# Mixture-of-experts stage: groups ranked by size, the fullest group's two blocks on one set of weights, the smallest group's halves stacked

## The reference

```python
g_sel = argmax(hf @ w_r1 + b_r1)                 # one group of 4 per token
top_p, top_i = top_k(softmax(e_logits[g_sel]), 2) # two of its 4 experts
hid = silu(hf @ w_gate[e]) * (hf @ w_up[e])       # for every expert e, 1024 -> 256
hid = hid * combine[token, e]                     # zero where e was not chosen
out = sum over e of hid @ w_down[e]               # 256 -> 1024
x = x + out
```

## Time and profile before

| | us |
|---|---|
| median of 3 runs | 1083.11 (1082.84 to 1084.38) |
| profiled execution, its own time | 1084.64 |
| its span, first to last instruction | 1082.6 |
| PE busy in the span | 1070.2 (99%) |
| DVE busy | 726.8 (67%) |
| ACT busy | 617.7 (57%) |
| first product of pass 0 starts | 898.57 |
| transposes of pass 19 start | 1073.77 |

### The profile page before, as it was taken

One profiled execution on the slowest core, in us unless ns is written; L12 is line 12 of the kernel. 1 busy time (PEld: TensorE's weight loads), 2 busy tenths in 40 slices (PEclk: granted clock), 3 DMA queues, 4 the chain that ended last, 5 costly groups with the idle time before them and its releaser, 6 DMA issues.

```text
span 1082.6 us, 17152 instructions
## 1 busy us (share of the span) xinstructions
PE 1070.2 (99%) x7044; PEld 957.6 (88%) x7044; DVE 726.8 (67%) x814; ACT 617.7 (57%) x731; POOL 50.2 (5%) x41
## 2 busy tenths in 40 slices
PE   9999999999999999999999999999999999999997
PEld 7998889999989999998898777889999978878886
DVE  7954665865766544545765648895455678899995
ACT  7653369674465444443673437775444467877773
POOL 0600100000000000000000000000000002000000
PEclk9999999999999999999999999999999999999999
DMA  8552254554655555555346433434446457999992
GB/s 314 196 187 77 87 183 167 204 211 170 229 179 196 196 194 194 194 192 196 117 156 215 159 98 112 156 120 154 163 161 230 160 200 274 356 378 381 364 402 92
DMA packets 31921, 216.92 MB, mean 200 GB/s; under 512 B 4304, under 2 KB 4560, under 8 KB 6384
## 3 DMA queue, kind: packets, MB, share of 16 engines
q1 hardware_dynamic: 29824, 211.93, 54.9%
q0 software_dynamic: 1616, 2.66, 0.7%
q10 hardware_dynamic: 416, 1.39, 0.3%
HBM read 215.44 MB, written 3.67 MB: 202 GB/s over the span
## 4 chain that ended last, share of the span: by engine, by line
PE 93%; DVE 5%; ACT 1%; issue 1%; DMA 0%; POOLq 0%; DVEq 0%; ACTq 0%
PE bank L567 28%; PE bank L569 28%; PE bank L568 27%; PE bank L628 2%; DVE wlo L1642 1%; PE bank L1039 1%; PE bank L961 1%; PE bank L943 1%; DVE last_lo L1642 1%; DVE wlo L1645 1%; PE bank L709 0%; PE bank L688 0%; PE bank L874 0%; PE bank L1091 0%; PE bank L706 0%
## 5 line engine op out<-in xcount | busy, mean ns | idle before, releaser
L1645 DVE TENSOR_TENSOR wlo<-raw,whi 128x2048 fp32r<-128x2048 f32 x138 | 317.7, 2307 | 167.8 <-ACT whi L1125 167.6
L1125 ACT ACTIVATE whi<-raw 128x2048 fp32r<-128x2048 f32 (+1 forms) x168 | 319.4, 1906 | 134.9 <-PE bank L569 132.7
L567 PE MATMUL bank<-normedT_hi,whi 128*128 128x256 f32 x640 | 177.6, 278 | 0.0
L568 PE MATMUL bank<-normedT_lo,whi 128*128 128x256 f32 x640 | 177.0, 277 | 0.0
L569 PE MATMUL bank<-normedT_hi,wlo 128*128 128x256 f32 x640 | 177.0, 276 | 0.0
L1125 ACT ACTIVATE buf<-bank 128x512 f32<-128x512 f32 (+5 forms) x147 | 70.9, 526 | 156.7 <-PE bank L569 128.1
L567 PE MATMUL bank<-xT_hi,whi 128*128 128x256 f32 (+1 forms) x448 | 127.1, 284 | 0.8 <-issue 0.8
L568 PE MATMUL bank<-xT_lo,whi 128*128 128x256 f32 (+1 forms) x448 | 126.3, 282 | 0.0
L569 PE MATMUL bank<-xT_hi,wlo 128*128 128x256 f32 (+1 forms) x448 | 126.3, 282 | 0.0
L567 PEld LDWEIGHTS bank<-normedT_hi,whi 128*128 128x128 f32 x640 | 120.2, 188 | 1.0 <-issue 0.6
L568 PEld LDWEIGHTS bank<-normedT_lo,whi 128*128 128x128 f32 x640 | 120.2, 188 | 0.7 <-issue 0.2
(11 more groups left out here) (396 smaller groups left out, 2227.1 us busy)
## 6 DMA issues: line engine op xcount, KB each, us to landing
raw<-weights_dram SPq DMA_DIRECT2D x175, 1024.0 KB, 5.0
buf<-weights_dram SPq DMA_DIRECT2D x24, 1024.0 KB, 8.0
buf<-x_dram SPq DMA_DIRECT2D x2, 512.0 KB, 4.1
buf<-mem_dram ACTq DMA_DIRECT2D x1, 1024.0 KB, 8.9
token_rows<-buf SPq DMA_DIRECT2D x1, 1024.0 KB, 8.6
buf<-final_w_dram POOLq DMA_DIRECT2D x1, 512.0 KB, 3.8
con<-consts_dram SPq DMA_DIRECT2D x1, 486.0 KB, 8.8
buf<-small_w_dram SPq DMA_DIRECT2D x1, 432.0 KB, 11.4
```

The lines of the kernel that those rows point to most:

```text
L567: E.matmul(out_, lh, rh, start=start, stop=False)
L568: E.matmul(out_, lh, rl, start=False, stop=False)
L1125: return S.activation(out_, in_, func, **kw)
L1645: V.tensor_tensor(wlo[:, n % SLOTS, :], raw[:, n % SLOTS, :], whi[:, n % SLOTS, :].bitcast(f32), sub).then_inc(piece_split, 1)
```

## The change

**Ranking.** The groups are ranked by their token counts on the chip: rank 0 is the fullest, rank 3 the smallest. Rank 0 has blocks 0 and 1, rank 1 block 2, rank 2 block 3, and rank 3 block 4, in which only 64 slots are taken (the smallest of four groups of 256 tokens has at most 64). All expert pieces now have addresses that follow from the ranking (`ORDER`), so SP waits for `indexed` before it loads any of them. The store of `token_rows` is issued before them.

**Order of passes.** Passes 0 to 11 are four triples. In triple t, passes 3t and 3t + 1 run blocks 0 and 1 with the same expert of rank 0 (pieces loaded and split once), and pass 3t + 2 runs block 4 with an expert of rank 3. Passes 12 to 15 are block 2, 16 to 19 block 3. In all 48 pieces are loaded and split, against 60.

**Stacked passes.** In block 4 the stationary operand is 128 columns that hold the 64 high parts beside the 64 low parts. One matmul with `whi` gives high by high in rows 0 to 63 and low by high in rows 64 to 127; a second one, with 64 stationary columns, adds high by low to rows 0 to 63. That is 24 matmuls per pass against 36. ACT then copies rows 64 to 127 (`FOLD`), DVE adds them, and the sums of the block are folded in the same way at the end (`fold_sums`, `own_added`).

**Halves.** Pieces are copied and split in halves of 1024 columns; the first piece's load is in two halves as well. Two up banks, 6 and 7, alternate, and the transposes go into the same bank as the pass's up product. `xb` gathers are 320 columns wide; three of them now stand ahead of pass 0. The order on PE is `first(p)`, `turn(p - 1)`, `second(p)`, `down(p - 1)`, where first and second are the two halves of `expert_up`.

The core of the diff (constants and order of passes, SP, PE, then ACT, then DVE; `feed_halves` stands on ACT and on DVE, where it waits for ACT's half and subtracts):

```diff
+def expert_of(p):
+    return 2 * (p // 3) + (p % 3 == 2) if p < TRIPLES else p - 4
+def leaves_weights(p):
+    return p >= TRIPLES or p % 3 > 0
+STEPS = []
+for _p in range(PASSES):
+    STEPS.append(("first", _p))
+    if _p:
+        STEPS.append(("turn", _p - 1))
+    STEPS.append(("second", _p))
+    if _p:
+        STEPS.append(("down", _p - 1))
+STEPS += [("turn", PASSES - 1), ("down", PASSES - 1)]
+        if leaves_weights(_p):
+            LEFT.append(AT[_use])
+            USED_AT[AT[_use]] = M0 + len(LEFT)
-FOURTH = AT[1, 4]
+FOURTH = 6
+def freed_by(u):
+    return LEFT[u - SLOTS if u < FOURTH else u - SLOTS - 1]
...
+            sp.wait_ge(squares, squares_ahead["z"] + 2 * RT)
+            sp.dma_start(token_rows.rearrange("(r p) c -> p r c", p=P), X).then_inc(rows_stored, 16)
+            sp.wait_ge(indexed, 1)
+                if rank not in group_at:
+                    group_at[rank] = sp.value_load(ORDER[0:1, rank:rank + 1], min_val=M0, max_val=M0 + 3 * (EXPERTS - EXPERTS // GROUPS))
+                if u >= RAWS:
+                    sp.wait_ge(half_split, 2 * (u - RAWS) + 2)
...
+                    if k % 2 == 0:
+                        pe.wait_ge(half_split, 2 * u + k // 2 + 1)
+                    pair_, high_ = XG[0][:, 4 * half + k, at:at + P], XG[0][:, 4 * half + k, at:at + HALF]
+                    if not ends:
+                        E.matmul(b[:, :], pair_, w[0][:, k, :], start=begins, stop=False, skip_group_check=True)
+                    last = E.matmul(b[0:HALF, :], high_, w[1][:, k, :], start=False, stop=False, skip_group_check=True)
...
+            gather_rest(0, 3)
+            for step, p in STEPS:
+                elif step == "second":
+                    expert_up(p, 1)
+                    if p == 0:
+                        spread_slots()
+                        gather_rest(3, 5)
+                    if p == 1:
+                        gather_rest(5, 8)
...
+            def feed_halves(n):
+                    if u == FOURTH:
+                        act.wait_ge(gathered, 4 + KT)
+                    elif u < SLOTS:
+                        act.wait_ge(pieces_used, M0 + u + 1 - SLOTS)
+                    else:
+                        act.wait_ge(pieces_used, USED_AT[freed_by(u)])
+                    A(WHI[split_of(u)][:, half], RAW[raw_of(u)][:, half], ACT.Copy).then_inc(half_high, 1)
...
+                up_over(act, p)
+                b, n = up_bank(p), P
+                if stacked(p):
+                    A(FOLD, b[HALF:P, :], ACT.Copy).then_inc(fold_copied, 1)
+                    feed_halves(2)
+                    act.wait_ge(fold_summed, p // 3 + 1)
+                    b, n = FOLD, HALF
...
+            for step, p in STEPS:
+                if step == "second":
+                    expert_silu(p)
...
+                    feed_halves(5 if p >= TRIPLES else 2 if stacked(p) else 3)
+                    if p == 12:
+                        fold_sums()
+                elif step == "turn":
+                    act.wait_ge(moe_turned, p + 1)
...
+                        A(HTS[0].rearrange("p f s -> p (f s)"), up_bank(p)[:, 0:2 * P], ACT.Copy).then_inc(high["moe"], 1)
+                        feed_halves(1)
...
+                if stacked(p):
+                    dve.wait_ge(fold_copied, p // 3 + 1)
+                    V.tensor_tensor(FOLD, FOLD, b[0:HALF, :], add).then_inc(fold_summed, 1)
+                    feed_halves(1)
+                    b, n = FOLD, HALF
...
+            feed_halves(LEAD - 4)
+            for step, p in STEPS:
+                if step == "second":
+                    expert_hidden(p)
...
+                    feed_halves(5 if p >= TRIPLES else 3)
+                    if p - 1 in (9, 10, 11, 15):
+                        own_added(block_of(p - 1), p - 1)
+                elif step == "turn":
+                    hidden_low(p)
+                    if not stacked(p):
+                        feed_halves(1)
```

More of the change, by code:

```diff
@@ L1 @@
 from contextlib import ExitStack
+import itertools
 import numpy as np
@@ L41, with rank_of, member_of, block_of @@
 SLOTTED = BLOCKS * P
+HALF = P // 2
+SMALL = GROUPS
+TAKEN = SMALL * P + HALF
 SHARED = 12
 M0 = PB["moe"]
[L44 to L48, removed]
+TRIPLES = 12
+LEAD = 6
+def expert_of(p):
+    return 2 * (p // 3) + (p % 3 == 2) if p < TRIPLES else p - 4
+def rank_of(e):
+    return 3 * (e % 2) if e < 8 else e // 4 - 1
+def member_of(e):
+    return e // 2 if e < 8 else e % 4
+def block_of(p):
+    return (0, 1, SMALL)[p % 3] if p < TRIPLES else p // 4 - 1
+def stacked(p):
+    return block_of(p) == SMALL
+def leaves_weights(p):
[9 more added lines that the diff above has]
+STEPS += [("turn", PASSES - 1), ("down", PASSES - 1)]
+KIND = {"first": 0, "second": 1, "down": 2}
+USES, AT, USED_AT, LEFT = [], {}, {}, []
+for _step, _p in STEPS:
+    if _step != "turn":
+        _use = (KIND[_step], expert_of(_p))
+        if _use not in AT:
+            AT[_use] = len(USES)
+            USES.append(_use)
+        if leaves_weights(_p):
+            LEFT.append(AT[_use])
+            USED_AT[AT[_use]] = M0 + len(LEFT)
 NU = M0 + len(USES)
@@ new lines, in _ @@
+            release(V.scalar_tensor_tensor(sizes_, bank("tot")[:, 0:GROUPS], float(GROUPS), slot_const("tie"), mult, add), "tot")
+            moved(dve, "tot")
+            chain(V.tensor_tensor(bigger, bc1(sizes_, GROUPS), bc(sizes_, GROUPS), ALU.is_gt))
+            chain(V.tensor_reduce(ranked, bigger, AX.X, add))
+            V.scalar_tensor_tensor(block_at, ranked, 1.0, ranked, amin, add)
+            chain(V.tensor_tensor(of_rank, bc1(ranked, GROUPS), bc(slot_const("group"), GROUPS), ALU.is_equal))
@@ L2239, in _ @@
+            dve.wait_ge(counted, 2)
+            for r in range(RT):
+                ins = V.scalar_tensor_tensor(own[:, r, :], block_at, float(P), counts[:, r, :], mult, add)
+            release(ins, "cum")
+            chain(V.tensor_tensor(of_rank, of_rank, bc1(slot_const("piece"), GROUPS), mult))
             moved(dve, "cum")
-            chain(V.tensor_reduce(mine, own, AX.X, add))
-            V.scalar_tensor_tensor(extra, mine, P + 0.5, spare, ALU.is_gt, mult)
-            chain(V.tensor_tensor(own[:, :, 0], mine, first_slot, add))
+            V.tensor_reduce(ORDER[:, 0:GROUPS], of_rank, AX.X, amax).then_inc(indexed, 1)
@@ L2243, in _ @@
+            chain(V.tensor_tensor(own, own, group, mult))
+            chain(V.tensor_reduce(slot, own, AX.X, add))
             iota = slot_const("iota")
-            for r in range(RT):
-                last = V.tensor_scalar(PICK[:, r, 0:2 * P], iota[:, 0:2 * P], extra[:, r:r + 1], own[:, r, 0:1], sub, ALU.is_equal)
-            last.then_inc(slotted, 1)
-            chain(V.tensor_tensor(slot, own[:, :, 0], extra, add))
-            for r in range(RT):
-                last = V.tensor_scalar(PICK[:, r, 2 * P:], iota[:, 2 * P:], slot[:, r:r + 1], None, ALU.is_equal)
@@ L2250, in _ @@
-            last.then_inc(slotted, 1)
+            for at, n in ((0, 2 * P), (2 * P, SLOTTED - 2 * P)):
+                for r in range(RT):
+                    last = V.tensor_scalar(PICK[:, r, at:at + n], iota[:, at:at + n], slot[:, r:r + 1], None, ALU.is_equal)
+                last.then_inc(slotted, 1)
             V.tensor_tensor(gsh, gl, bc(gmx, 4), sub).then_inc(route_max, 1)
```

334 lines of the change are left out of this document (174 added, 160 removed).

## The result

| | before | after |
|---|---|---|
| median of 4 runs, us | 1083.01 (1082.84 to 1084.38) | 1093.66 (1092.31 to 1096.07) |
| profiled execution, its span | 1082.6 | 1090.9 |
| first gather to first product of pass 0 | 3.90 | 8.08 |
| first product to transposes of pass 19 | 175.20 | 179.09 |
| transposes of pass 19 to the end | 8.8 | 9.8 |

The change made the kernel slower: ratio 1.0098, 95% interval 1.0078 to 1.0118, 10.65 us. The forecast was 1083.8, with a range up to 1089.5, and 1093.66 lies above it.

The account below looks back on a forecast made before the run. PE was taken to bound the kernel, with DVE just behind. Start 4.8, PE's work -13.8, new waits +11.9 and earlier waits -2.2 gave +0.7 on the median 1083.11, so 1083.8 us; range 1076.5 to 1089.5.

Parts of the forecast that it names:

- the sum: Whole kernel: start 4.8, PE's work -13.8, new waits 11.9, less 2.2 of earlier waits, gives +0.7 us.
- The start: Ahead of pass 0: DVE's ranking operations and first half split are late, so first(0) starts at 903.3, 4.8 us later.
- a sign of being wrong: First three pieces: ACT waiting for a load there would show the forecast wrong on the slow side.
- The waits: PE ahead of downs and first(2): late split buffers and DVE's and ACT's in-order queues make it wait 11.9 us together.
- The price of a wait: PE's pauses: the 11.9 us of waits were counted as idle time, with nothing known to fill them.
- The clock of 1.00: Expert stage before the change: the granted clock was read as 1.00 in the windows.
- PE's work: First product to turn(19): fewer matmuls and narrower gathers cut PE's sum from 173.0 to 159.2, 13.8 us less.
- The tail: What follows turn(19): taken to be the same in both kernels, so left out of the comparison.
- Width switches cost nothing: Stacked passes: about 94 alternations between 128 and 64 stationary columns were taken as costing zero, since the matmuls are fp32r.
- The rival at 1098: Stacked passes: each width switch drains the engine, 94 x 0.15 is 14 us, giving 1098; chance 0.07.
- DVE is the bound: Passes 12 to 19: halves at 1.28 lengthen each pass by 0.5, 4 us, giving 1087.8; chance 0.23, shared with a later start.
- DVE never behind: Waits ahead of first(2) and in passes 10, 12, 16: the 5.5 us from DVE's queue vanish, giving 1078.3; chance 0.28.

Follow-up runs that it names:

- e6: Changed kernel with its first five pieces loaded from fixed addresses ahead of the ranking; 1092.97 us, ratio 1.0076 to the kernel before.
- e2: Changed kernel with halves that wait for a late buffer moved behind the hidden values' copy and low part (passes 0, 1, 4, 7, 10); 1083.64 us, ratio 0.9996.
- e4: Changed kernel with late halves, own_added and the small block's fold copy all moved behind the hidden values' copy and low part; 1081.58 us, ratio 0.9979.
- e5_again: The changed kernel itself, unedited, run again for more executions; 1095.70 us, ratio 1.0101 to the kernel before.
- e1: Changed kernel with matmuls of zeros on PE during its waits ahead of first(0), down(1), down(10) and down(12); 1090.23 us, ratio 1.0057.
- e3: Changed kernel with only own_added (four places) and the small block's fold copy moved behind the hidden values' copy and low part; 1087.14 us, ratio 1.0034.
- e8: e4 plus earlier gathers and first split, one half later, small block's additions spread over passes 12 to 15, zeros ahead of first(0); 1077.46 us, ratio 0.9936.
- e9: e8 with the last three gathers' copies and low parts behind hidden_low(0), and the extra half behind hidden_low(2); 1077.15 us, ratio 0.9925.
- e12: e9 with a handmade DVE delay ahead of down(7) and eleven matmuls of zeros on PE inside that pause; 1082.31 us, ratio 0.9975.

## Why the prediction was wrong, step by step

Working from the transposes of the routing logits to the end of the span in the two profiled executions: 192.6 before (from 890.03), 201.9 after (from 888.98), 9.35 more where the sum said 0.7. The other 1.3 of the 10.65 lies outside these two stretches: the median of the change is 0.6 above its profiled execution, and that of the kernel before 1.6 below its own, of which 1.05 stand ahead of the stretch compared here.

- **The start, +4.8: right.** Measured +4.5. 8.08 from the first gather to `first(0)` where 8 was said (and 903.3 less 898.57 is 4.7, not 4.8). DVE is what is late, and e6 confirms that the load doesn't set `first(0)`. But ACT did wait for the load, 0.31, 0.20 and 1.44 for the first two pieces, which the prediction had named as a sign of being wrong; where the clock is full it costs PE 0.4 to 0.7 in pass 0.
- **The waits, 11.9: right, one by one.** Predicted and measured ahead of `down(0)` 1.1 and 1.06, `first(2)` 0.7 and 0.68, `down(1)` 3.05 and 3.00, `down(4)` 0.75 and 1.01, `down(7)` 0.75 and 0.73, `down(10)` 1.9 and 1.93, `down(12)` 3.05 and 2.71, `down(16)` 0.6 and 0.43; sum 11.55. e2 to e4 show the cause that was given.
- **The price of a wait: the step that failed.** "Together 11.9. Nothing I know fills them" priced a pause at its idle time, and so did the start. By the trace two of these pauses (1.93 and 2.71) and the 1.33 ahead of `first(0)`, and in e5_again a fourth (2.99), have a slow stretch at 1.2 GHz behind them: 4.8 here, 4.4 by e1. With the 2.1 for restarts (next point) a price of pauses that the sum lacks makes 6.9 of the 8.65 that it is off in these two traces. The clock of 1.00 was read in the earlier trace rows and then taken as given for a kernel that pauses, though before, PE never paused for more than 1.1. The Trainium skill, TensorE: Matmul & The Clock Gate, section Why this matters for your kernels, warns against idle gaps between bursts of matmuls, since the clock falls to half behind them; it was not weighed. The traces agree in kind and not in size: slow stretches stand behind pauses of 1.33 and 1.93 too, which are shorter than the gaps that it names, and the pause of 3.00 ahead of `down(1)` has one in e5_again and e6 and none in the first profile and e3.
- **PE's work, -13.8: too large by 3.5.** First product to turn(19), 179.09, less 11.55 of waits and 4.8 of clock, is 162.7 and not 159.2. The stacked matmuls stand 0.2315 apart and not 0.2265 (0.5 in all). A restart after a wait costs about 0.27 beside the idle time: at `down(1)` 0.16 more than the wait to the first matmul and 0.11 more to the second, eight times, 2.1. The transposes of the stacked passes, 64 x 64 each, take 0.25 more than those of 128 x 128, in four passes, 1.0. Together 3.6.
- **The tail, "the same in both kernels": wrong by 1.0.** The last store is issued 3.97 before the end of the span, 2.9 before. The last block is now a full group's and no longer the surplus; that its store takes longer because of its rows was not tested.
- **Width switches cost nothing: right.** The stacked matmuls keep their distance, with the 0.5 above. The rival at 1098 is nearer to the time than the forecast, but by luck: between these matmuls no drain is seen. Whether the 0.25 at the 64 x 64 transposes is one stays open.
- **DVE is the bound (1087.8): half right.** The turns of passes 13 to 16 come 8.4 apart, as before; but e3 and e4 show that the additions do exceed DVE's slack where they stand close together, 1.4 at `down(13)`. The rival's price was wrong too: six halves at 1.28 with 0.48 and 0.42 make 8.6 of 8.45, about 1 us over eight passes and not 4.
- **DVE never behind (1078.3): wrong for this kernel.** e8 and e9 come to about that time (1077.46, 1077.15), but by a mended order that removes other waits too.

The ledger: waits -0.35, clock +4.8, work +3.5, start -0.3, tail +1.0, together 8.65 on top of 0.7. Had the pauses cost their idle time alone, the sum would have been short by 1.8 and the time within the range.

## What to carry to other kernels

Price a new wait of a dense matmul stage at more than its length: here 12.9 us of pauses (the eight of 11.55 and the 1.33 ahead of `first(0)`) cost about 19.8, with the restarts and the slow clock behind some of them. Before taking work from the busiest engine, look at what its in-order partners have queued ahead of the one short operation that it will then wait for; here moving the short operation ahead (e4) was worth 12.9 us by the ratios, more than the 48 matmuls that the change removed (10.9). If a pause can't be avoided, matmuls of zeros into a bank that is PE's own anyway kept the clock up in e1 and e12.

## What was not expected of the hardware

- The slow stretch is not certain. Over the thirteen profiles with the changed order of passes, 12 of 26 pauses of 1.3 to 4.2 us have one behind them: 3 of 13 of those up to 1.8 us, 9 of 13 of the longer ones. From the first gather to the last transposes no slow stretch stands anywhere else, and none behind a shorter pause. The same pause has it in one execution (2.99 at `down(1)` in e5_again) and not in another (3.00 in the first profile). Its slow distances add up to 2.6 to 5.1 us, and it costs 1.6 to 2.7. The Trainium skill, TensorE: Matmul & The Clock Gate, says in its Part 1 that how many matmuls run slow at a kernel's start varies from run to run, with the phase of the clock gate. It says so of the start; the traces show the like behind pauses.
- Its distances are those of the two levels: 0.427 between 512-column matmuls at 1.2 GHz, 0.2265 to 0.2315 at 2.4.
- A slow stretch stands also between 120 and 140 us (clock 0.91) in the profiled execution of before, where PE is recorded as busy for 20.00 of 20, in small products and transposes without a wait of note; in that of after it is absent. So the two spans can't be compared from their first instruction. The kernel before itself spreads by 3 to 4 us (1083.01 to 1087.34 in 23 executions); how much of that such stretches make is not shown.
